# A two-layer decoder step: LayerNorm by halves of the tokens with the additions in another order, weight remainders and first fetches moved

## What is computed

```python
for l in range(DEPTH):                                   # DEPTH = 2
    mix_p, (ckv_p, kpe_p, tail_p, _) = token_mixer(xp, ...)   # pooling, latent attention, gated MLP
    xp = layernorm(ALPHA * xp + mix_p, ln1_g[l], ln1_b[l])
    ffn_p, conv_tail_p = conv_ffn(xp, ...)
    xp = layernorm(ALPHA * xp + ffn_p, ln2_g[l], ln2_b[l])
    ...                                                  # the same for the new tokens xs

def layernorm(x, g, b):
    mu = jnp.mean(xf, axis=-1, keepdims=True)
    xc = xf - mu
    var = jnp.mean(xc * xc, axis=-1, keepdims=True)
    return (xc * lax.rsqrt(var + LN_EPS) * g + b).astype(x.dtype)

def conv_ffn(h, prefix, w_up, conv_w, conv_b, w_down):
    a = h @ w_up
    ext = jnp.concatenate([prefix.astype(a.dtype), a], axis=1)
    c = conv_b + conv_w[0] * ext[:, 0:T]
    for k in range(1, CONV_W):                           # CONV_W = 3
        c = c + conv_w[k] * ext[:, k:k + T]
    gate, up = jnp.split(c, 2, axis=-1)
    y = (jax.nn.silu(gate) * up) @ w_down
```

## Time and profile before

| | |
|---|---|
| median of 3 runs | 2403.9 us (2401.56 to 2406.0) |
| the profiled execution's own time | 2401.4 us, span of its trace 2399.6 us |
| mean granted TensorE clock | 0.968 of full |
| busy: PE (TensorE) | 2265.4 us, 94% |
| busy: DVE (VectorE) | 1252.1 us, 52% |
| busy: ACT (ScalarE) | 894.1 us, 37% |
| busy: POOL (GpSimd) | 284.2 us, 12% |
| DMA | 250.40 MB, mean 104 GB/s |

### The profile page before, as it was taken

How to read it: one execution, slowest core, us unless ns; L and a number is a source line. 1 busy time by engine, 2 the same in 40 slices (tenths; PEclk the granted TensorE clock), 3 DMA queues, 4 the chain that set the end, 5 groups by cost and what they waited for, 6 DMA issues and landing times.

```text
span 2399.6 us, 43196 instructions
## 1 busy us (share of the span) xinstructions
PE 2265.4 (94%) x17458; PEld 2060.1 (86%) x17458; DVE 1252.1 (52%) x2038; ACT 894.1 (37%) x1626; POOL 284.2 (12%) x285
## 2 busy tenths in 40 slices
PE   7989998999998999999999999989999889999997
PEld 7966666699997899999888666667999888999996
DVE  4744443433457773566667444334333677626664
ACT  4334343433335431334343343334233354313333
POOL 0022220000015000000240222100000240000002
PEclk9989998899999999999999899988999999999998
DMA  6245550022252322225333455300223422322251
GB/s 223 79 148 172 171 179 1 1 72 86 79 170 75 96 86 93 70 79 174 113 108 107 148 178 173 125 1 11 87 80 98 153 80 88 102 76 73 85 186 51
DMA packets 68366, 250.40 MB, mean 104 GB/s; under 512 B 8272, under 2 KB 13264, under 8 KB 68112
## 3 DMA queue, kind: packets, MB, share of 16 engines
q1 hardware_dynamic: 45360, 164.79, 21.3%
...
HBM read 243.69 MB, written 4.90 MB: 104 GB/s over the span
## 4 chain that ended last, share of the span: by engine, by line
PE 83%; DVE 7%; issue 3%; POOLq 2%; ACT 2%; DMA 1%; DVEq 1%; another core or an unknown queue 0%; ACTq 0%; SPq 0%
PE PS L930 55%; PE PS L1123 5%; PE PS L1147 5%; PE PS L1167 5%; PE PS L1136 2%; DVE m_WL L1339 2%; POOLq L446 2%; PE PS L1276 1%; PE PS L1153 1%; PE PS L1254 1%; DVE m_X L1371 1%; DMA m_WS<-in_w_units 1%; PE PS L1265 1%; PE PS L961 1%; DVE m_XL L1379 1%
## 5 line engine op out<-in xcount | busy, mean ns | idle before, releaser
L930 PE MATMUL PS<-m_XH,m_WH 128*128 128x288 f32 x2560 | 734.9, 299 | 47.4 <-DVE m_WL L1339 29.5
L930 PE MATMUL PS<-m_XL,m_WH 128*128 128x288 f32 x2560 | 726.5, 297 | 0.0
L930 PE MATMUL PS<-m_XH,m_WL 128*128 128x288 f32 x2560 | 584.5, 298 | 0.0
L930 PEld LDWEIGHTS PS<-m_XH,m_WH 128*128 128x128 f32 x2560 | 487.1, 190 | 55.0 <-DVE m_WL L1339 37.0
L1339 DVE TENSOR_TENSOR m_WL<-m_WS,m_WH 128x1024 fp32r<-128x1024 f32 (+2 forms) x284 | 369.4, 1302 | 245.3 <-ACT m_WH L506 235.1
L930 PEld LDWEIGHTS PS<-m_XL,m_WH 128*128 128x128 f32 x2560 | 487.5, 190 | 0.8
L506 ACT ACTIVATE m_WH<-m_WS 128x1024 fp32r<-128x1024 f32 (+2 forms) x284 | 315.4, 1113 | 314.1 <-PE PS L930 293.6
L930 PEld LDWEIGHTS PS<-m_XH,m_WL 128*128 128x128 f32 x2560 | 425.7, 190 | 0.0
L930 PE MATMUL PS<-m_HH,m_WH 128*128 128x288 f32 x704 | 206.2, 300 | 5.5 <-DVE m_HL L1339 5.5
L930 PE MATMUL PS<-m_HL,m_WH 128*128 128x288 f32 x704 | 204.7, 299 | 0.0
L491 POOL DMA_INDIRECT m_RAW<-in_cache_rows,m_IDXS x128 | 122.6, 958 | 542.8 <-PE PS L1167 240.2
...
## 6 DMA issues: line engine op xcount, KB each, us to landing
...
m_RAW<-in_cache_rows,m_IDXS POOLq DMA_INDIRECT x128, 5.3
...
m_CST<-in_consts SPq DMA_DIRECT2D x1, 1425.5 KB, 13.5
...
```

The costliest lines, as they stand in the source:

```text
L930: mm = pe.matmul(out(half), w(part, k), x(k)[:, half_of(half)], start=(k == 0 and part == 0 and x is xh), stop=(k == last and part == 1))
```

## The change

Six edits, in the order of the program:

1. First fetches. SyncE fetches weight unit 0 ahead of X, and the second halves of X and the constants (1425.5 KB) behind the units 3 to 5. ScalarE issues the page table and the parameters after its first copies instead of ahead of them. The split of X's half 1 (`XH`, `XL`) moves into `first_halves`, where `normal_hi` and `normal_lo` do it for n = -1; so ScalarE no longer waits for X's half 1 before it reads PE's first tiles out. The page rows (`page_rows`) move to the fourth tile of `w_in`.
2. GpSimd's `norm`: all squares of half 0 come ahead of all sums of half 1.
3. The last tiles of half 1 are summed on PE: X's tile 7 gets a ones-matmul of its own behind XS (6 adds on GpSimd instead of 7), the squares' tiles 6 and 7 as well (5 adds instead of 7); the square sum stands before k = 0 of a = 3.
4. `half_passes` on PE runs u = 0 and u = 1 up to their last k but one, and then the last k of both.
5. `up_tile` with `halved` (j = 0, 2, 4 in the first FFN half): the remainder of each weight unit of j + 1 is made after the first tap.
6. `up_tile` with `last` (the last j of the FFN): the remainder of `w_down`'s second unit comes behind HL.

```diff
+            fetch(0, U_INA, W_IN + IN_FIRST[0], D)
             for c in range(4):
                 k = slice(2 * c, 2 * c + 2)
                 sp.dma_start(X[:, k, 0:HT], x_t[:, k, 0:HT]).then_inc(S[f"x_in{c}"], 16)
-                if c in (0, 2):
-                    fetch(0, U_INA + c // 2, W_IN + IN_FIRST[c // 2], D)
...
                 for k in range(DT):
                     sum_up(0, k)
-                sum_up(1, 0)
-                sum_squares(0, 1)
-                sum_up(1, 1)
-                for k in (2, 3, 4):
-                    sum_squares(0, k)
-                sum_up(1, 2)
-                for k in (5, 6, 7):
+                for k in range(1, DT):
                     sum_squares(0, k)
-                for k in range(3, DT):
+                for k in range(DT - 1):
                     sum_up(1, k)
                 if not last:
-                    for k in range(1, DT):
+                    for k in range(1, DT - 2):
                         sum_squares(1, k)
...
+                mm = pe.matmul(PS[:, 4 + half, 0:HT], C["ones"], XS[:, h], start=True, stop=(half == 0))
+                if half == 1:
+                    pe.wait_ge(S["mm_free1"], CREDIT["mm_free1"] + l * NM + m0 + 8)
+                    mm = pe.matmul(PS[:, 4 + half, 0:HT], C["ones"], X[:, DT - 1, h], start=False, stop=True)
...
+                mm = pe.matmul(PS[:, 6 + half, 0:HT], C["ones"], SS[:, h], start=True, stop=(half == 0))
+                if half == 1:
+                    pe.wait_ge(S["n_sq"], ln(n, half))
+                    for k in (DT - 2, DT - 1):
+                        mm = pe.matmul(PS[:, 6 + half, 0:HT], C["ones"], LSQ[:, k, h], start=False, stop=(k == DT - 1))
...
+                for u in range(2):
+                    pe.wait_ge(S["w_lo"], l * NU + u0 + u + 1)
+                    pe.wait_ge(S[f"mm_free{u}"], CREDIT[f"mm_free{u}"] + l * NM + m0)
+                    halves(range(kts - 1), (0,), weights_of(SPLIT_OF[u0 + u]), xh, xl, lambda half: PS[:, 2 * u, 0:HT], kts - 1,
+                           (lambda k: pe.wait_ge(S[parts], before + k + 1)) if u == 0 else None)
+                pe.wait_ge(S[parts], before + kts)
+                for u in range(2):
+                    halves((kts - 1,), (0,), weights_of(SPLIT_OF[u0 + u]), xh, xl, lambda half: PS[:, 2 * u, 0:HT], kts - 1)\
+                        .then_inc(S[f"mm_done{u}"], 1)
...
-                    among = {0: (4, lambda: feature_sum(n, 1)), 3: (1, lambda: square_sum(n, 1))}.get(a) if n >= 0 else None
+                    among = {0: (4, lambda: feature_sum(n, 1, *ended)), 3: (0, lambda: square_sum(n, 1))}.get(a) if n >= 0 else None
...
+                        if halved:
+                            weight_lo_in_loop(u0 + 2 + par, par, width)
...
-                    weight_lo_in_loop(u0 + 3, 1, width)
+                    if not halved and not last:
+                        weight_lo_in_loop(u0 + 3, 1, width)
                     dve.wait_ge(S["h_hi"], n0 + 1)
                     at = HL[:, j, :] if isinstance(j, int) else tile(HL, j)
                     lo(at, HX[:, :], HH[:, j, :] if isinstance(j, int) else tile(HH, j)).then_inc(S["h_lo"], 1)
+                    if last:
+                        weight_lo_in_loop(u0 + 3, 1, width)
```

More of the change, by code:

```diff
@@ L383, in _ @@
                 sp.dma_start(X[:, k, 0:HT], x_t[:, k, 0:HT]).then_inc(S[f"x_in{c}"], 16)
-                if c in (0, 2):
-                    fetch(0, U_INA + c // 2, W_IN + IN_FIRST[c // 2], D)
-            fetch(0, U_INA + 2, W_IN + IN_FIRST[2], D)
-            for c in range(2):
-                k = slice(4 * c, 4 * c + 4)
-                sp.dma_start(X[:, k, HT:T], x_t[:, k, HT:T]).then_inc(S["x_in_b"], 16)
-            sp.dma_start(CST[:, :], consts).then_inc(S["consts"], 16)
             for l in range(DEPTH):
-                for a in range(3 if l == 0 else 0, 6):
-                    if a == 2:
+                for a in range(1 if l == 0 else 0, 6):
+                    if a == 2 and l > 0:
                         sp.wait_ge(S["stored"], l * N_STORES * 16)
@@ L438, in sum_up @@
                     ins = pool.drain()
-                    if k == DT - 1:
+                    if k == (DT - 1, DT - 2)[half]:
                         ins.then_inc(S["n_xs"], 1)
@@ L446, in sum_squares @@
                     ins = pool.drain()
-                    if k == DT - 1:
+                    if k == (DT - 1, DT - 3)[half]:
                         ins.then_inc(S["n_sqs"], 1)
@@ L526, in _ @@
                     weight_hi(U_INA + (0, 1, 2)[(k + 1) // 4])
-            act.wait_ge(S["x_in_b"], 32)
-            for k in range(DT):
-                copy(XH[:, k, HT:T], X[:, k, HT:T]).then_inc(S["x_hi"], 1)
-                if k == 3:
-                    weight_hi(U_INA + 3)
-            act.wait_ge(S["params"], 16)
+            act.dma_start(PTB[:, :], page_table.rearrange("b n -> (b n)").partition_broadcast(P))\
+                .then_inc(S["table"], 16)
+            act.dma_start(PARS[:, :], params.rearrange("p l n -> p (l n)")).then_inc(S["params"], 16)
+            weight_hi(U_INA + 3)
             def squares(n, half, ks):
@@ L547, in normal_hi @@
                 for k in ks:
+                    if n < 0:
+                        act.wait_ge(S["x_in_b"], 32)
+                        copy(XH[:, k, h], X[:, k, h]).then_inc(S["x_hi"], 1)
+                        continue
                     act.wait_ge(S["n_xn"], ln(n, half, k + 1))
@@ L1375, in normal_lo @@
                 if n == 2 * DEPTH - 1:
+                    return
+                if n < 0:
+                    split_in(half, k)
                     return
@@ L1805, in _, with up_tile @@
                     dve.memset(EB[:, par, 0:2], 0.0)
-                def up_tile(hf, j, width):
+                def up_tile(hf, j, width, halved=False, last=False):
                     n0 = (l * 2 + hf) * FH + j
@@ L1832, in up_tile @@
                             dve.drain().then_inc(S["c_ready"], 1)
[L1833 removed]
+                            if not halved:
+                                weight_lo_in_loop(u0 + 2, 0, width)
                     dve.drain()
@@ L1851, in _ @@
                     for j in range(first):
-                        up_tile(hf, j, D)
+                        up_tile(hf, j, D, halved=j in UP_FIRST)
                     with dve.Fori(first, FH - 1) as j:
                         up_tile(hf, j, D)
-                    up_tile(hf, FH - 1, UW)
+                    up_tile(hf, FH - 1, UW, last=hf == 1)
                     if hf == 0:
```

113 lines of the change are left out of this document (56 added, 57 removed).

## The result

The changed kernel took 2372.55 us, the median of 4 runs (2370.94 to 2374.5); the kernel before, beside it on the same chip, 2403.09 (2401.56 to 2406.0). That is 30.5 us less; the ratio is 0.9872, 95% interval 0.9855 to 0.9889. I had predicted 2368, with a range of 2358 to 2381. The profiled execution took 2374.5 us, its span is 2372.7.

A forecast was written before the change was run, and what follows sets the result against it. It took PE, busy 94% of the span, as the bound, its waits for GpSimd's square sum foremost. Terms summed to -34.5 us, giving 2366.9 from the profiled 2401.4 or 2369.4 from the median 2403.9; forecast 2368, range 2358 to 2381.

The forecast's parts named there:

- Squares of half 0 first: In the norms, PE's wait for GpSimd's square sum goes or nearly goes: -6.3 us twice (n = 0, 2), -7.5 twice (n = 1, 3).
- First fetches: At the start, PE's 3.9 us wait at 20.2 and the half clock behind it go: -5.5 us, bounds -2 and -7.
- Last tiles on PE: Half 1's last sums in the norms move to PE: +0.6 us twice, +0.1 for n = 1, -0.5 at the end.
- the earlier sum helps nobody: In norms n = 0 and 2, an earlier feature sum gains nothing, as VectorE starts half 1's centring only later.
- w_out: Interleaving u = 0 and 1 behind w_out makes PE idle 2.05 us: +0.4 and 0.1, twice; bounds 0 and 2 each.
- w_down: Interleaving behind w_down with HL first lengthens PE's wait from 2.8 to 3.6 us: +0.9 twice; lower bound -0.65.
- Remainders ahead of the taps: In the up projection, PE's waits for weight remainders fall from about 8.9 to 6.4 us: -2.5 twice, bounds -1 and -4.4.
- (a): Rival: in the norms the square adds still end late, leaving 2 us of wait with a clock drop; 2376 us, chance 0.12.
- (b): Rival: the clock stays up behind the first norm's a = 0, in the tail and in j = 2, 4; 2360, chance 0.15.
- (c): Rival: the start gains nothing, PE being held by units 5 to 7 behind constants; 2374 us, chance 0.1.
- (d): Rival: slower, as new idle places at projection starts, a = 0 and up projection end in half clock; 2411, chance 0.02.
- (e): Rival: the norm's 4.9 us wait isn't due to GpSimd's order, so the change does nothing there; 2397 us, chance 0.03.

The follow-up runs named there:

- e1: The kernel before with only GpSimd's squares of half 0 moved ahead of all sums of half 1: 2375.97 us, ratio 0.9899.
- e10: Second run of e2's kernel (changed kernel, u = 0 and 1 in plain order, w_down's remainder ahead of HL): 2355.84 us, ratio 0.9802.
- e9: The kernel before with only squares first, last tiles summed on PE and remainders ahead of the taps: 2361.8 us, ratio 0.9833.
- e2: The changed kernel with u = 0 and 1 in plain order and w_down's second remainder ahead of HL again: 2356.97 us, ratio 0.9825.
- e3: The changed kernel with the weight remainders of j = 1, 3 and 5 behind the taps again: 2373.47 us, ratio 0.9896.
- e5: The changed kernel with u = 0 and 1 interleaved behind w_down only, its second remainder ahead of HL again: 2356.91 us, ratio 0.9804.
- e6: The kernel of e5 with TensorE's loop over the up projection's pairs of tiles written out: 2356.46 us, ratio 0.9803.
- e7: The kernel before with only the first fetches changed, including X's later half 1 split and page rows: 2397.64 us, ratio 0.9984.
- e11: Second run of e7's kernel, the kernel before with only the first fetches changed: 2395.54 us, ratio 0.9977.
- e8: The kernel before with only the last tiles of half 1 summed on PE, its square sum one k earlier: 2398.56 us, ratio 0.9993.
- e12: The kernel before, unchanged, run again for a second trace: 2402.08 us, ratio 0.9996.
- e4: The changed kernel, run once more without further change: 2363.92 us, ratio 0.9859.

## Why the prediction was right, point by point

The total was right, 30.5 us where 34.5 were summed, because its largest terms were: the norm's four. Of the smaller ones several were mis-sized, in both directions, and that they and the stretches that no edit touches came out near the forecast together is luck. The steps u = 12 to 15 moved up with u = 11 to within 0.2 us in all four norms, the sign that the prediction had named.

- **Squares of half 0 first, -6.3 twice and -7.5 twice.** Measured 6.1 and 7.8 / 7.7, shown by e1 alone. The chain of reasons holds too: the adds at 1.17 beside VectorE, no wait for n = 1 and 3, VectorE the next in line for n = 0. The last add ended at 721.00, which is 720.2 on the clock of the kernel before, where I had 719.5 to 719.8, and 0.66 of wait stayed. By the rule of the Trainium skill, "SBUF — State Buffer" (Who interferes with whom), I had estimated 720.1 and 0.4, and that came nearer than my reading of the rows. That one engine is blocked for a whole instruction isn't shown by this alone: the second add also began 0.8 after the first, at ScalarE's pace.
- **First fetches, -5.5.** Measured 5.3 at the first pooled tile (5.3 to 7.0 in the nine traces that have the edit, 0.3 to 1.3 in the four without it), 6.0 by e10 against e9. The total is right, the parts aren't, and that they cancel is luck: "PE's start stays" was wrong, its first matmul came at 8.37 instead of 11.11, since unit 0 has landed when X's first two tiles have (ScalarE copies it at 6.02 instead of 8.74); the waits of 1.2 at 11.6 and 3.3 at 30.4 are new. The latter is ScalarE's queue, in its timeline of the changed kernel (`m_Z` is a tile of PE read out):

```profile
29.57 1.06 ACT L499 ACTIVATE m_WH<-m_WS 128x1024 fp32r<-128x1024 f32 x1 [4.00 <-DMA m_WS<-in_w_units]
30.53 0.76 ACT L499 ACTIVATE m_XH<-m_X 128x288 fp32r<-128x288 f32 x2
31.20 1.04 ACT L499 ACTIVATE m_WH<-m_WS 128x1024 fp32r<-128x1024 f32 x1
32.14 1.09 ACT L499 ACTIVATE m_XH<-m_X 128x288 fp32r<-128x288 f32 x3
33.14 0.39 ACT L499 ACTIVATE m_Z<-PS 128x288 f32<-128x288 f32 x1
```

  The tile is read out at 33.14 only, behind a weight unit that landed at 29.57, another one and five copies of X's half 1. I had such a meeting at 42 us, at 0.8, and 0.4 for the copies. The size of this wait varies: 3.3 and 2.6 us in the changed kernel and e10, at most 0.7 in e2, e3, e5, e6, e7 and e11.
- **Last tiles on PE, +0.6, +0.6, +0.1 and -0.5.** Wrong sign. The step that failed is "the earlier sum helps nobody": PE stood 1.9 us for it and the clock was 0.76 behind that wait, so all that PE does next, the square sum too, came later. Measured: about -1.1 twice at the first tap (1.3 to 1.5 against 0.0 to 0.5), which without edit 5 is lost again by j = 6 (e8), and 3.9 at the end. Of that 3.9, 2.8 is the clock of the sums at the end, which I had as the alternative of -3.5. It shows in VectorE's idle time ahead of the last variance, 5.04 in the first trace of the kernel before and 2.2 in all nine with the edit. The rows of the kernel before, of e12 and of e8:

```profile
2389.88 0.46 DVE L1361 TENSOR_SCALAR m_RN<-PS 128x288 f32<-128x288 f32 x1 [5.04 <-PE PS L981]
2388.18 0.46 DVE L1361 TENSOR_SCALAR m_RN<-PS 128x288 f32<-128x288 f32 x1 [2.22 <-PE PS L981]
2383.21 0.46 DVE L1370 TENSOR_SCALAR m_RN<-PS 128x288 f32<-128x288 f32 x1 [2.23 <-PE PS L990]
```

  Without the edit it is 2.2 in e7 and e12 as well, 3.7 in e1 and 3.9 in e11. The edit's own share is 1.1, and the high clock came with it nine times out of nine. The Trainium skill, "TensorE: Matmul & The Clock Gate" (What's actually happening), says that how many matmuls run cold differs from run to run in the same kernel; these ends agree, 0 to 2.8 us without any edit of it.
- **w_out, +0.5 twice.** The wait was right (2.2 for 2.05), its consequence mis-sized: 0.8 without a drop of the clock, 2.5 with one, and that came in four of six. I had this as the upper bound of 2 each; for the sum it should have been the likely case.
- **w_down, +0.9 twice.** The wait is 3.6 as predicted, 0.84 more; the stage lost 1.1 to 1.3 in six of six. But e10, in the plain order, lost 1.2 in both layers too, with a drop of the clock, and the plain order elsewhere 0.0 to 0.1 with a drop, or won 1.2 to 1.3 without. So the loss of 0.9 each can't be told from the clock's by these runs. The lower bound (-0.65 without edit 6) was wrong: e5 shows the shorter wait, and in the second layer the 0.7 that eats it.
- **Remainders ahead of the taps, -2.5 twice.** The mechanism held, the term is 4 to 5: the waits fall from 8.3 to 4.7, not to 6.4 (e4 has 4.3 in a window that leaves out one of 0.5, as e3 has 7.8). I had given j = 2, 4 and 6 new waits of 0.7 to 1.3; the trace has one of 0.5, and the old ones of 1.9, 2.4, 2.5 and 1.0 became none, 1.7, 2.1 and none. In the changed kernel 2.7 and 2.2 of it arrived at j = 6, and "up b" lost 2.8 and 2.4, as it did in traces without the edit (up to 3.0).
- **What was in no term**: about 11 us of stretches that no edit touches (attention -3.6 and -2.3, "up b" -2.8 and -2.4) in the first trace of the changed kernel. They can't be laid on the change (for the first attention a part stays open, see e9): e12 has -2.0, -2.5 and -2.5 of them without any edit, and e4, the same kernel, lost 3.6 in its first layer and won 3.8 in its second. The two traces differ by 26.9 us; without these stretches the stages with edits come to 37, and 1 more lies in the stretch that the table leaves out.

Rivals: (a) fell: an add took 1.17, not 1.6, and 0.66 us of wait stayed. (b) held in part, at the end and behind a = 0. (c), (d) and (e) fell.
